# A fourth Strassen step pair in every second feed-forward chunk of a hybrid decoder layer, with the chunks written out

## The reference

```python
h = rms_norm(x, g_ffn)
x = x + (jax.nn.silu(h @ w_gate) * (h @ w_up)) @ w_down
return rms_norm(x, g_final)
```

## Time and profile before

| | us |
|---|---|
| median of 3 runs (1197.28 to 1198.63) | 1198.25 |
| the profiled execution's own time | 1197.7 |
| its span, first to last instruction | 1196.0 |
| TensorE busy in the span | 1184.9 (99%) |
| VectorE busy | 930.3 (78%) |
| ScalarE busy | 673.6 (56%) |

### The profile page before, as it was taken

How to read it: one execution, slowest core, us unless ns; L and a number is a source line. 1 busy time by engine, 2 the same in 40 slices (tenths; PEclk the granted TensorE clock), 3 DMA queues, 4 the chain that set the end, 5 groups by cost and what they waited for, 6 DMA issues and landing times.

```text
span 1196.0 us, 16405 instructions
## 1 busy us (share of the span) xinstructions
PE 1184.9 (99%) x5421; PEld 982.6 (82%) x5421; DVE 930.3 (78%) x1171; ACT 673.6 (56%) x881; POOL 83.6 (7%) x89
## 2 busy tenths in 40 slices
PE   9999999999999999999999999999999999999997
PEld 7888888888888888888888888888888888888885
DVE  5755555557855666999899899989989889978886
ACT  5665555445744575756556555655555554545553
POOL 0042332200210000000000000000000000000000
PEclk9999999999999999999999999999999999999999
DMA  9865455556556544466666566566655666665663
GB/s 340 296 211 173 162 175 177 174 176 222 166 187 185 191 158 141 159 212 186 202 197 205 176 210 225 166 202 198 209 187 199 213 211 203 211 216 174 200 206 141
DMA packets 65851, 234.52 MB, mean 196 GB/s; under 512 B 7696, under 2 KB 8464, under 8 KB 65424
## 3 DMA queue, kind: packets, MB, share of 16 engines
q1 hardware_dynamic: 63072, 225.60, 57.6%
q10 hardware_dynamic: 2736, 8.35, 1.8%
HBM read 231.83 MB, written 2.10 MB: 196 GB/s over the span
## 4 chain that ended last, share of the span: by engine, by line
PE 93%; DVE 4%; DMA 1%; ACT 1%; issue 1%; SPq 0%; POOLq 0%; POOL 0%; ACTq 0%; DVEq 0%
PE ps L489 24%; PE ps L491 24%; PE ps L490 24%; PE ps L732 6%; PE ps L734 6%; PE ps L733 6%; DVE wlo L1624 2%; PE ps L521 1%; DMA raw<-w_stream 1%; DVE alo L1282 0%; PE ps L604 0%; DVE wlo L1270 0%; PE ps L559 0%; PE ps L564 0%; PE ps L688 0%
## 5 line engine op out<-in xcount | busy, mean ns | idle before, releaser
L1145 ACT ACTIVATE whi<-raw 128x1024 fp32r<-128x1024 f32 (+1 forms) x309 | 303.5, 992 | 216.6 <-PE ps L491 91.5
L1624 DVE TENSOR_TENSOR wlo<-raw,whi 128x1024 fp32r<-128x1024 f32 (+1 forms) x309 | 345.5, 1137 | 25.1 <-ACT whi L1145 24.3
L1270 DVE TENSOR_TENSOR wlo<-raw,whi 128x1024 fp32r<-128x1024 f32 x160 | 198.4, 1245 | 110.9 <-ACT whi L893 110.7
L489 PE MATMUL ps<-whi,ahi 128*128 128x512 f32 x600 | 235.6, 393 | 0.0
L491 PE MATMUL ps<-whi,alo 128*128 128x512 f32 x600 | 233.7, 390 | 0.0
L490 PE MATMUL ps<-wlo,ahi 128*128 128x512 f32 x600 | 233.5, 389 | 0.0
L893 ACT ACTIVATE whi<-raw 128x1024 fp32r<-128x1024 f32 x160 | 168.4, 1058 | 106.9 <-PE ps L491 94.0
L489 PE MATMUL ps<-whi,bhi 128*128 128x512 f32 x448 | 180.0, 402 | 1.5 <-DVE blo L1363 1.0
L491 PE MATMUL ps<-whi,blo 128*128 128x512 f32 x448 | 175.1, 391 | 0.0
L490 PE MATMUL ps<-wlo,bhi 128*128 128x512 f32 x448 | 174.5, 389 | 0.0
L491 PEld LDWEIGHTS ps<-whi,alo 128*128 128x128 f32 x600 | 112.6, 188 | 23.7
(11 more groups left out here) (244 smaller groups left out, 1488.1 us busy)
## 6 DMA issues: line engine op xcount, KB each, us to landing
raw<-w_stream SPq DMA_DIRECT2D x422, 512.0 KB, 4.1
res<-x_in ACTq DMA_DIRECT2D x4, 512.0 KB, 7.9
stage<-mem_in ACTq DMA_DIRECT2D x4, 512.0 KB, 6.1
proj<-mem_T ACTq DMA_DIRECT2D x2, 1024.0 KB, 7.8
stage<-x_T SPq DMA_DIRECT2D x7, 256.0 KB, 7.5
y_out<-res SPq DMA_DIRECT2D x4, 320.0 KB, 3.0
raw<-w_stream SPq DMA_DIRECT2D x4, 256.0 KB, 4.8
gfin<-g_final ACTq DMA_DIRECT2D x1, 1024.0 KB, 4.8
```

The source lines that it names most:

```text
L489: nc.tensor.matmul(bank, lhsT=a_h, rhs=w_h, start=start, stop=False)
L1145: nc.scalar.activation(whi_here, src, ACT.Copy).then_inc(hi_ready, 1)
L1270: vec.tensor_tensor(tile_pair(wlo, j), tile_pair(raw, j), tile_pair(whi, j).bitcast(f32), ALU.subtract).then_inc(lo_ready, 1)
L1624: vec.tensor_tensor(lo_here, src, hi_here.bitcast(f32), ALU.subtract).then_inc(lo_ready, 1)
```

## The change

Of every two chunks the odd-numbered one (1, 3, 5, 7, 9) takes step s = 3 of gate and up as a fourth quad too. Its order is G4 G5 S0 G6 S1 G7 S2 U4 U5 S3 U6 U7: 24 places, 180 matmuls. The even chunks keep their order. Two tables, FFN (places) and FFN_TILES (tiles of the stream), are made in plain Python, and PE, ACT, DVE and SP are written out from them without hardware loops. SP's waits follow the places: wsum frees a quad's first tile, the split of part 2 its second, a plain split its own. p1_copy, combine and Silu stand at places 18, 19, 21 in even chunks (before: 17, 18, 21) and at 20, 21, 23 in odd ones. The activation sums are made for four steps instead of three: the four DVE operations of s_forms grow from 384 to 512 columns, ACT casts two more pieces to araw and s3h of 512 columns, and s_lows gets one more operation of 512 columns (s3l). araw and asum grow accordingly.

```diff
+FORMS = QUADS + 1
+FFN_ORDER = ("G3 G4 G5 S0 G6 G7 S1 U3 S2 U4 U5 U6 U7", "G4 G5 S0 G6 S1 G7 S2 U4 U5 S3 U6 U7")
+for c in range(NFC):
+    CHUNK_AT.append(len(FFN))
+    for name in FFN_ORDER[c % 2].split():
+        kind, s = name[0], int(name[1:])
+        if kind == "S":
+            q = len([1 for place in FFN if place[4] == 0])
+            last_quad = len(FFN)
+            FFN += [(len(FFN_TILES), kind, s, q, part) for part in range(QUAD_PARTS)]
+            FFN_TILES += [(c, 0, s), (c, 1, s)]
+        else:
+            FFN.append((len(FFN_TILES), kind, s, None, None))
+            FFN_TILES.append((c, "GU".index(kind), s))
+    LAST_QUAD_AT.append(last_quad)
-UNITS_AT, P1_AT, COMBINED, SILU_AT = 2, 17, 18, 21
+UNITS_AT = 2
+P1_AT, COMBINED, SILU_AT = (18, 20), (19, 21), (21, 23)
...
+            for i, (r, kind, s, q, part) in enumerate(FFN):
+                if part == 1:
+                    sp.wait_ge(w_sums, 3 * q + 3)
+                elif part == 2:
+                    r += 1
+                    sp.wait_ge(lo_ready, J_FF + i + 1)
+                elif part is None:
+                    sp.wait_ge(lo_ready, J_FF + i + 1)
+                else:
+                    continue
+                j = J_FF + r + RING
+                if j < J_DN:
+                    sp.dma_start(tile_pair(raw, j), stream[j]).then_inc(w_loaded[j % RING], 16)
...
                 def s_form(f):
+                    if n == QUADS:
+                        return [b[:, f, :] for b in (s3h, s3l)]
...
-            chunk(0)
-            with pe.Fori(0, (NFC - 1) // PAIR) as i:
-                for c in range(1, PAIR + 1):
-                    chunk(c, i * PAIR)
+            for c in range(NFC):
+                chunk(c)
...
-                    if U_H3 <= u < U_H3 + QUADS:
+                    if U_H3 <= u < U_H3 + FORMS:
...
+            nc.scalar.activation(s3h[:], asum[:, :, QUADS], ACT.Copy).then_inc(s_hi, 1)
...
+                vec.tensor_tensor(sfl[:], asum[:, 1:QUAD_PARTS, 0:QUADS], sfh[:].bitcast(f32), ALU.subtract)
+                vec.tensor_tensor(s3l[:], asum[:, :, QUADS], s3h[:].bitcast(f32), ALU.subtract).then_inc(s_lo, 1)
```

More of the change, by code:

```diff
@@ L61 @@
 QUADS = 3
+FORMS = QUADS + 1
 QUAD_PARTS = 4
-QUAD_AT = (3, 9, 14)
 CHUNK_RAW = 2 * SPG
[L65 to L70, removed]
+FFN_ORDER = ("G3 G4 G5 S0 G6 G7 S1 U3 S2 U4 U5 U6 U7", "G4 G5 S0 G6 S1 G7 S2 U4 U5 S3 U6 U7")
+FFN = []
+FFN_TILES = []
+CHUNK_AT = []
+LAST_QUAD_AT = []
+for c in range(NFC):
[11 more added lines that the diff above has]
+    LAST_QUAD_AT.append(last_quad)
+CHUNK_AT.append(len(FFN))
+FFN_SUMS = 3 * len([1 for place in FFN if place[4] == 0])
+V_DN = J_FF + len(FFN)
 DOWN_QUADS = 8
@@ L261, in build @@
         fat = [shared]
+        fourth_at = [fat[0] + 4 * (FF // P - 2 * KS) * SEQ]
+        s3h = sb("s3h", [P, QUAD_PARTS, P], f32r, at=fourth_at)
+        s3l = sb("s3l", [P, QUAD_PARTS, P], f32r, at=fourth_at)
         fhi = sb("fhi", [P, FF // P, SEQ], f32r, at=fat)
+        assert fourth_at[0] <= fat[0]
         flo = sb("flo", [P, FF // P, SEQ], f32r, at=fat)
@@ L354, in unit_bank @@
             return 6 if u % 2 == 0 else 7 if u < U_FF - 1 else 1
[L356 to L364, removed]
         @block.sync
@@ L385, in _ @@
                     sp.dma_start(tile_pair(raw, s), stream[i * RING + s]).then_inc(w_loaded[s], 16)
[L386 to L393, removed]
+            for j in range(RING):
+                sp.wait_ge(lo_ready, J_FF + j - RING + 1)
+                sp.dma_start(tile_pair(raw, j), stream[J_FF + j]).then_inc(w_loaded[j], 16)
+            for i, (r, kind, s, q, part) in enumerate(FFN):
[11 more added lines that the diff above has]
+                    sp.dma_start(tile_pair(raw, j), stream[j]).then_inc(w_loaded[j % RING], 16)
             for j in range(RING):
@@ L737, in quad_weights, with quad_part @@
                 return ([b[:, v % RING, half * GC:(half + 1) * GC] for b in (whi, wlo)] for half in range(2))
-            def quad_part(c, ci, n, part):
-                v = J_FF + c * CHUNK + QUAD_AT[n] + part
-                opens, closes = n == 0, n == QUADS - 1
+            def quad_part(c, i):
+                v, (r, kind, n, q, part) = J_FF + i, FFN[i]
+                opens, closes = n == 0, i - part == LAST_QUAD_AT[c]
                 left, right = quad_weights(v)
@@ L769, in quad_part, with chunk @@
                 done.then_inc(step_used, 1)
[L771 to L783, removed]
+            def chunk(c):
+                for i in range(CHUNK_AT[c], CHUNK_AT[c + 1]):
+                    p, (r, kind, s, q, part) = i - CHUNK_AT[c], FFN[i]
                     if c == 0 and p == 1:
@@ L789, in chunk @@
                     if c > 0 and p == UNITS_AT:
[L790 to L794, removed]
+                        ffn_unit(2 * (c - 1))
+                        ffn_unit(2 * (c - 1) + 1)
+                    if kind == "G":
                         if p == 0:
-                            bank_free(G_FF + 2 * c, ci)
+                            bank_free(G_FF + 2 * c)
@@ L797, in chunk @@
                         if c == 0:
                             pe.wait_ge(unit_lo, U_H3 + s + 1)
[L799 to L806, removed]
@@ L808, in ffn_unit @@
-            def ffn_unit(n, ci):
-                await_out(pe, G_FF + 1 + 2 * (n // 2), ci)
-                pe.wait_ge(unit_lo, ci * 2 + (U_FF + n - 1))
+                        step(J_FF + i, 0, KS * s, ahi, alo, G_FF % 2, p == 0, False)
+                    if kind == "S":
+                        if part == 0 and s == 0:
+                            bank_free(G_FF + 2 * c + 1)
+                            if c == 0:
+                                pe.wait_ge(s_lo, 1)
+                                pe.wait_ge(unit_lo, U_FF - 2)
+                        quad_part(c, i)
@@ L812, in ffn_unit @@
+                    if kind == "U":
+                        opens = "U" not in [place[1] for place in FFN[CHUNK_AT[c]:i]]
+                        if opens:
+                            pe.wait_ge(unit_lo, U_FF + 2 * c)
+                        step(J_FF + i, 0, KS * s, ahi, alo, (G_FF + 1) % 2, (False, opens), s == SPG - 1)
+            def ffn_unit(n):
+                await_out(pe, G_FF + 1 + 2 * (n // 2))
+                pe.wait_ge(unit_lo, U_FF + n - 1)
                 unit(U_FF + n, fact, KS * (n % 2))
-            chunk(0)
@@ L859, in _ @@
                 if i == LEAD:
-                    ffn_unit(2 * (NFC - 1), 0)
-                    ffn_unit(2 * (NFC - 1) + 1, 0)
+                    ffn_unit(2 * (NFC - 1))
+                    ffn_unit(2 * (NFC - 1) + 1)
                 if i == FIRST_QUAD[0]:
@@ L1124, in _, with part_cast @@
             act.wait_ge(s_made, 1)
[L1125 to L1129, removed]
+            nc.scalar.activation(ahi[:, 0:KS * QUADS:KS, P:2 * P], asum[:, 0, 0:QUADS], ACT.Copy)
+            nc.scalar.activation(sfh[:], asum[:, 1:QUAD_PARTS, 0:QUADS], ACT.Copy)
+            nc.scalar.activation(s3h[:], asum[:, :, QUADS], ACT.Copy).then_inc(s_hi, 1)
+            def part_cast(v, j, part, sums):
                 whi_here, src = whi[:, v % RING, :], tile_pair(raw, j)
                 if part is None or part == 0:
-                    act.wait_ge(w_loaded[j % RING], loaded_by(j, jt))
+                    act.wait_ge(w_loaded[j % RING], loaded_by(j, 0))
                 if part == 0:
-                    act.wait_ge(w_loaded[(j + 1) % RING], loaded_by(j + 1, jt))
+                    act.wait_ge(w_loaded[(j + 1) % RING], loaded_by(j + 1, 0))
                 if part in (2, 3):
@@ L1143, in part_cast, with chunk_cast @@
                     whi_here, src = whi_here[:, GC:KS * GC], src[:, GC:KS * GC]
-                act.wait_ge(step_used, vt + (v - RING + 1))
+                act.wait_ge(step_used, v - RING + 1)
                 nc.scalar.activation(whi_here, src, ACT.Copy).then_inc(hi_ready, 1)
[L1147 to L1151, removed]
+            def chunk_cast(i):
+                if i < len(FFN):
+                    r, kind, s, q, part = FFN[i]
+                    part_cast(J_FF + i, J_FF + r, part, 0 if part is None else 3 * q)
+                else:
+                    down_cast(i - len(FFN))
             def down_cast(i):
@@ L1184, in gate @@
                 done.then_inc(silu_ready, 1)
[L1186 to L1208, removed]
+            for c in range(NFC):
+                for p in range(CHUNK_AT[c + 1] - CHUNK_AT[c]):
+                    chunk_cast(CHUNK_AT[c] + p + LEAD)
+                    if c == 0 and p == 2:
+                        for u in (SPG - 2, SPG - 1):
+                            unit(U_H3 + u, KS * u, C_FFN, ahi)
+                    if c == 0 and p == 6:
+                        await_out(act, G_FF - 1)
+                        token_squares(3, 0, res, junk1[:])
+                    if c == 0 and p == 8:
+                        token_squares(3, 1, res, junk1[:])
+                    if p == P1_AT[c % 2]:
```

(71 more changed lines are left out.)

50 lines of the change are left out of this document (23 added, 27 removed).

## The result

| | before | after |
|---|---|---|
| median, us | 1197.86 | 1206.18 |
| runs | 1197.28 to 1198.63 | 1205.22 to 1206.85 |
| ratio | | 1.0067, interval 1.0051 to 1.0083 |
| span of the profiled execution | 1196.0 | 1203.9 |

What follows compares the result with a forecast made beforehand. PE was taken to bound the feed-forward chunks, with DVE 9% behind. Five pairs at +3.0 and the start at +1.1 gave +4.1 on the profiled 1197.7, 1201.8, forecast as a median of 1202.3; range 1196.9 to 1207.5.

Steps and rivals of the forecast that it cites:

- The pair of chunks: Feed-forward chunks, an odd one and the even one behind it: +0.6 us a pair, +3.0 for five pairs.
- S0's part 3: Even chunk: its weights come at 12.65 where PE wants them at 12.3, so PE waits 0.35.
- the ledger: Step-by-step times of the odd chunk from PE's first matmul: chunk and handover take 42.65 against 42.40, +0.25.
- DVE "above 97%": Sign expected in the trace after: DVE busy above 97% in the odd chunks.
- combine is one place later: Even chunks: combine moves one place later with four plain steps behind it; put at 0.
- the fourth quad: Odd chunks: costs DVE 4.09 us more each and saves PE 0.68; net +3.0 over five pairs.
- The start: Activation sums ahead of the first chunk: s_forms 0.53 and s_lows 0.60 longer on DVE, +1.1 us.
- ACT's two pieces to araw: Start: among ACT's three more pieces, held hidden by its idle time; 1 us more if the cover were gone.
- Writing the code out: Feed-forward chunks without hardware loops: no branch cost seen, fetches few; taken as 0, bounds 0 and +1.
- the rule weighed as a rival: Feed-forward loops: taken branches break instruction prefetch, so writing out would help; chance 0.01 of another rival's 0.08.
- likeliest case: Whole kernel: the forecast alone, +2.4 to +7 us, 1200.6 to 1205; chance 0.45.
- The third rival: Odd chunks: S2's tile lands after 4.2, lateness carries on; pair +1.8 to +2.3, kernel 1208.4 to 1210.9; chance 0.13.

Runs made afterwards that it cites:

- short tiles: Changed kernel, but in odd chunks the second tile of S2 and S3 loaded only to an eighth, the rest stale: 1199.37, -6.8.
- new order: Changed kernel with SP's waits mended, odd chunks reordered to G4 G5 S0 G6 G7 S1 U4 S2 U5 S3 U6 U7: 1201.55, -2.4 against experiment 3.
- experiment 5: Experiment 1 (written out, three quads everywhere) with activation sums made for four steps: 1203.35, +2.3 over experiment 1.
- experiment 3: Changed kernel with SP skipping the waits that have no transfer to issue: 1203.92, -2.3 against the changed kernel.
- experiment 6: Experiment 3 with the fourth step's activation sums made late in chunk 0: 1202.88, -1.0 against experiment 3.
- experiment 1: Chunks written out only, with three quads everywhere, three forms and old places, against the kernel before: 1201.05, +3.0.
- experiment 2: Experiment 1 with SP skipping the waits of the last four tiles' places, which have no transfer to issue: 1197.48, ratio 0.9994 to the kernel before.
- experiment 9: Kernel of the new order with combine of the odd chunks one place later (21 to 22): 1206.71, +5.2.
- experiment 4: Changed kernel with the 1 MB load of g_final issued some 32 places later in the w_down product: 1204.75, -1.4.

## Why the prediction was right, and where it was not

**The pair of chunks: right in mechanism, somewhat low.** Forecast +0.6, traced 3.87 / 5 = +0.77. In chunk 3, from its start at 619.7: S2 starts on DVE at 18.8 (forecast 18.7), its part 2 is usable at 24.1 (24.0), S3 starts at 29.2 (29.0), PE is at G3 at 43.1 (42.65). The split within the pair was wrong, and the total is near in part by luck. Odd chunks lost 0.56 each where +0.25 was forecast, even ones 0.22 where +0.35 was: S0's part 3, held to be 0.35 late there, is under 0.1 late. In the odd chunk S1's part 2, by the ledger 0.24 early (15.6 against 15.84), is 0.20 late in chunk 3, since S1 itself already waits for its second tile (0.32 on DVE): the ledger let a landing decide only from S2 on. Of the signs named, DVE "above 97%" in odd chunks did not come; it is busy 40.65 of chunk 3's 43.13 us, 94%, for it idles while the tiles land.

The short tiles and the new order, which leave DVE's work as it is, rule out that its amount alone decides, and point to the landing in a place freed late, as the forecast had it; that lighter traffic helped the short tiles is not ruled out. In the even chunks combine is one place later, which was put at 0 and not run by itself; four of the five even chunks lost at most 0.13, which bounds it. By the other reckoning, the changed kernel less experiment 5, the fourth quad is 2.8, near the forecast's 3.0. That differs from 3.87 in the main because SP's gap stands ahead of the last set of transposes in experiment 5 and not in the changed kernel.

By the Trainium skill's fit (SBUF — State Buffer, under its bandwidth curve), 2 us and the bytes at 436 GB/s, such a tile is an estimate of 3.2 us. In chunk 3 S2's tile, issued at 634.6, came at that (3.2); S3's, issued at 643.9 and 1.2 behind a neighbour, took 4.3. The fit counts bytes only; for S3's tile the measurement decides against it.

**The start: right in place, low in size.** Forecast +1.1, traced 1.5 to 1.6, by medians 2.3. The term counted DVE only, and held ACT's two pieces to araw to be hidden. They are not: they stand between ACT's casts to ahi, for which DVE waits. DVE's timeline, before and after (in the kernel after, the first two of the four operations are at 481.45, with 0.56 in their brackets):

```profile
481.26 1.66 DVE L1282 SCALAR_TENSOR_TENSOR alo<-ps,par,ahi 128x256 fp32r<-128x256 f32 x4 [0.56 <-ACT ahi L907]
```

```profile
482.91 0.88 DVE L1285 SCALAR_TENSOR_TENSOR alo<-ps,par,ahi 128x256 fp32r<-128x256 f32 x2 [0.58 <-ACT ahi L918]
```

The four ran in one go before and come in two pairs now, with a second wait of 0.58. DVE's next operation is 0.7 later by it (483.70 against 482.84, less the 0.2 from ahead of 439 us). With the 0.5 of s_forms and the 0.6 of s3l the split that releases PE near 502 is 1.8 later, not the 1.1 forecast; PE makes up 0.3 of that by the first set of transposes. The same second wait stands in experiments 3, 5 and 6, and in neither 1 nor before. The prediction had priced ACT's pieces at 1 us if their cover were gone; it is gone for the two to araw. Moving DVE's share away brought 1.0, near its 1.1. No run moved ACT's pieces alone.

**Writing the code out: the step that failed.** It was taken as 0, bounds 0 and +1, because the code was looked at for branches and fetches alone. Those are indeed nothing: 37 packets of q8 instead of 26, and experiment 2 within the noise of before. The +3.0 comes from a wait in SP's program that no longer has a transfer behind it. That SP's waits follow the places was in view; to see that the last four guard nothing, one had to run SP's list to its end. As for the rule weighed as a rival, that a taken branch to a target outside the pages at hand costs a fetch (the Trainium skill, Runtime: NRT & Kernel Launch, Instruction fetch mechanics): 0.9994 with 1 inside the interval shows no gain from writing out.

The change's price thus divides into 3.0 (SP), 2.3 (forms) and 2.8 (fourth quad) by medians, or 1.7, 3.9 and 2.3 of the span's 7.9 by milestones. Either way the parts are steps of one ladder and add up by construction, so the sum confirms nothing. That the time lies in the range although a term of 3.0 was put at 0 is luck: the room above was meant for later landings. With SP's waits mended the kernel is at 1203.92, within the likeliest case. The third rival's time, 1208.4, is near the measured one for another reason: S2's tile, which it has land after 4.2, landed in 3.2 in chunk 3.

## What to carry to other kernels

Work that saves the busiest engine time must be paid in the queue that feeds it; count by ring place and landing, not by sums of busy time. When a loop over an issuing queue is rewritten, walk its list through the last entries: a wait without a transfer behind it delays the next stage's first loads. And a late operation of one engine should be moved only after reading what is queued behind the instruction that waits for it (experiment 9).

## What was not expected of the hardware

Four 512 KB loads issued within 1.3 us landed after 3.7 to 6.2 us (median 5.0) in experiment 1; spread over 7.2 us in experiment 2 they took 3.3 to 4.6, and spread as much in the kernel before 3.3 to 5.4 (median 5.0), so the spread alone does not give the landing time. Two 512 KB loads issued 1.1 and 3.3 us behind a 1 MB load landed after 6.8 and 5.8, and without it after 3.1 and 3.3 (experiment 4). Ten chunks in loops and ten written out take the same time to within the noise.
